# Expert rows by indirect load: empty slots get an index beyond the table instead of row 0

## What is computed

```
g_sel = argmax(g_logits)                 # 1 of 4 groups
top_p, top_i = top_k(softmax(e_logits in that group), 2)
expert = g_sel * 8 + top_i               # 2 experts for each token
gate = t @ w_exp_gate[e]; up = t @ w_exp_up[e]
act = silu(gate) * up * w_tok
out = sum over e of act @ w_exp_down[e]
x = x + gt2 * out
```

## Time and profile before

| | |
|---|---|
| median of 3 runs | 851.57 us (849.39 to 853.31) |
| the profiled execution | 853.74 us |
| its span, first to last instruction | 852.0 us |
| mean granted TensorE clock | 0.93 |
| busy: PE, PEld, DVE, ACT, POOL | 736.1, 534.8, 264.0, 223.6, 97.4 us |
| moved by DMA | 195.88 MB |

### The profile page before, as it was taken

How to read it: one execution, slowest core, us unless ns; L and a number is a source line. 1 busy time by engine, 2 the same in 40 slices (tenths; PEclk the granted TensorE clock), 3 DMA queues, 4 the chain that set the end, 5 groups by cost and what they waited for, 6 DMA issues and landing times.

```text
span 852.0 us, 19975 instructions
## 1 busy us (share of the span) xinstructions
PE 736.1 (86%) x8393; PEld 534.8 (63%) x8394; DVE 264.0 (31%) x737; ACT 223.6 (26%) x523; POOL 97.4 (11%) x229
## 2 busy tenths in 40 slices
PE   2779999999985679999899899983898989989985
PEld 2567777776764457677676677732565656655543
DVE  0035413430135445555561112135111111111132
ACT  1331113123722431252254100151112122121125
POOL 7000000010101330000000000001222222222200
PEclk9769999999996888999999999976899999999996
DMA  7825679998443656315201706874899999999801
GB/s 259 229 96 198 230 261 330 325 327 303 101 115 91 157 150 183 114 51 173 51 26 39 295 0 259 334 295 180 309 411 411 414 413 413 414 412 414 346 14 55
DMA packets 108728, 195.88 MB, mean 230 GB/s; under 512 B 9964, under 2 KB 71097, under 8 KB 100488
## 3 DMA queue, kind: packets, MB, share of 16 engines
q1 hardware_dynamic: 106760, 189.94, 62.2%
q0 software_dynamic: 1920, 5.25, 1.7%
HBM read 185.40 MB, written 9.77 MB: 229 GB/s over the span
## 4 chain that ended last, share of the span: by engine, by line
PE 79%; DVE 7%; ACT 5%; issue 4%; DMA 4%; SPq 1%; DVEq 0%; ACTq 0%; POOLq 0%
PE ps L1110 17%; PE ps L520 10%; PE ps L1268 7%; PE ps L493 5%; PE ps L533 5%; PE ps L438 4%; PE ps L1052 4%; PE ps L417 3%; PE ps L496 3%; PE ps L421 2%; PE ps L483 2%; ACT arena L1496 1%; DMA arena<-in_w_ada 1%; PE ps L527 1%; PE ps L429 1%
## 5 line engine op out<-in xcount | busy, mean ns | idle before, releaser
L1110 PE MATMUL ps<-arena 128*128 128x288 f32 x576 | 144.0, 410 | 0.0
L1110 PEld LDWEIGHTS ps<-arena 128*128 128x128 f32 x576 | 108.9, 191 | 31.1 <-DMA arena<-in_w_in 0.9
L520 PE MATMUL ps<-arena 128*32 128x128 f32 x2432 | 86.5, 278 | 16.0 <-issue 14.0
L520 PEld LDWEIGHTS ps<-arena 128*32 128x32 f32 x2432 | 68.8, 111 | 40.5 <-issue 39.2
L1268 PE MATMUL ps<-arena 128*128 128x288 f32 x256 | 71.8, 425 | 4.1 <-ACT arena L1619 4.1
L1268 PEld LDWEIGHTS ps<-arena 128*128 128x128 f32 x256 | 47.5, 195 | 20.8 <-issue 8.8
L493 PE MATMUL ps<-level,arena 32*128 32x256 f32 x624 | 45.4, 406 | 0.5 <-DVE arena L760 0.5
L533 PE MATMUL ps<-arena,hact 128*32 128x256 f32 x608 | 40.7, 385 | 0.0
L391 POOL DMA_INDIRECT arena<-h_rows,idx_now x38 | 37.5, 987 | 9.5 <-issue 9.5
L755 DVE TENSOR_TENSOR h_row<-h_row,ps 128x64 f32<-128x64 f32 x38 | 8.4, 221 | 97.3 <-ACT h_row L614 97.3
L614 ACT ACTIVATE h_row<-ps 128x64 f32<-128x64 f32 x38 | 8.5, 223 | 111.2 <-PE ps L520 111.2
(11 more groups left out here) (433 smaller groups left out, 1030.7 us busy)
## 6 DMA issues: line engine op xcount, KB each, us to landing
arena<-in_w_exp_gate SPq DMA_DIRECT2D x32, 1024.0 KB
arena<-in_w_exp_up SPq DMA_DIRECT2D x32, 1024.0 KB
arena<-in_w_exp_down SPq DMA_DIRECT2D x32, 1024.0 KB
arena<-in_w_ada SPq DMA_DIRECT2D x12, 2048.0 KB, 10.3
arena<-in_w_in SPq DMA_DIRECT2D x18, 1024.0 KB, 5.7
arena<-in_w_ada_final SPq DMA_DIRECT2D x4, 2048.0 KB, 15.0
arena<-in_w_in SPq DMA_DIRECT2D x16, 512.0 KB
arena<-in_state_ssm_rec SPq DMA_DIRECT2D x8, 512.0 KB, 6.3
```

The source lines that it names most:

```text
L520: l = mm(ps[CW * q:CW * (q + 1), 5, 0:P].rearrange("p (g f) -> p g f", g=2), xwin[:, at:at + CW], gate_up[:, :, k, f:f + HF], start=(k == ...
L1110: l = mm(ps[:, 2 + 2 * sl + m, 0:TOK], w_ring[sl][:, k, m * P:(m + 1) * P], HN[:, k, :], start=(k == 0), stop=(k == KT - 1))
```

## The change

1. tid holds 288 - token, so that the sum of a slot with a token is 288 - token, and of an empty one still 0.
2. DVE computes slot_tab = 288 - sum first: token for a filled slot, 288 for an empty one. It waits for that (link), and computes idx = 4 * slot_tab + quarter from it. An empty slot's index is 1152 to 1155, beyond the last row, 1151.
3. The gather has a bounds_check of 1151 and doesn't take an index beyond it for an error.
4. POOL clears the two buffers once, ahead of y_row, since an empty slot's partition is now not written by a gather. In the first two gathers it holds zeros, and later what an earlier window left there; its weight is 0, and PT has no column 288.

```
-            link(g.iota(tid, pattern=[[0, 2], [P, 3]], base=0, channel_multiplier=1, allow_small_or_imprecise_dtypes=True))
+            link(g.iota(tid, pattern=[[0, 2], [-P, 3]], base=TOK, channel_multiplier=-1, allow_small_or_imprecise_dtypes=True))
...
             e.wait_ge(S("stored"), 16 * rec_stores[0])
+            for xg_ in xgs:
+                link(g.memset(xg_, 0.0))
             g.memset(y_row, 0.0).then_inc(S("y_row"), 1)
             g.memset(PT, 0.0).then_inc(S("pt"), 1)
...
-                g.indirect_dma_start(xgs[u], None, h2_rows, bass.IndirectOffsetOnAxis(rows, 0)).then_inc(S(f"xg_ld{u}"), 16)
+                g.indirect_dma_start(xgs[u], None, h2_rows, bass.IndirectOffsetOnAxis(rows, 0),
+                                     bounds_check=4 * TOK - 1, oob_is_err=False).then_inc(S(f"xg_ld{u}"), 16)
...
             e.wait_ge(S("count_mm"), 2)
-            ts(idx[:], ps[:, 6, 0:NWIN], 4.0, quarter, ALU.mult, ALU.add).then_inc(S("idx"), 1)
-            v.tensor_copy(slot_tab[:, 0, :], ps[:, 6, 0:NWIN])
+            link(ts(slot_tab[:, 0, :], ps[:, 6, 0:NWIN], -1.0, float(TOK), ALU.mult, ALU.add))
+            ts(idx[:], slot_tab[:, 0, :], 4.0, quarter, ALU.mult, ALU.add).then_inc(S("idx"), 1)
```

## The result

The changed kernel takes 855.88 us (median of 6 runs, 854.12 to 856.97) beside 851.05 us for the kernel before: ratio 1.0054, interval 1.0032 to 1.0075. By the ratio it is slower by 4.6 us (the two medians differ by 4.8). The profiled execution has a span of 855.2 us, against 852.0.

The account below looks back on a forecast made before the run. PE's own chain was taken to bound the loop, with the DMA running ahead. The terms 0.2 + 0.1 - 0.17 + 0.3 gave +0.4 us, put on the median as 852.0 us, range 848.5 to 855.8.

Parts of the forecast that it names:

- The loop is not held by the DMA: Loop over windows: the DMA is busy because it runs ahead; 2.9 MB less gather traffic gains nothing there.
- the first rival: Loop: the gathers' traffic held it back through the weights; 7.0 us less, 844.6 us, chance 0.06.
- The loop is PE's own chain: Loop: PE's own work sets the pace, 38 windows of 6.0 us each with the slow first one.
- whatever the check costs in the loop is hidden in POOL's idle time: Loop: extra gather cost from the check is hidden up to about 4.2 us in each window.
- Item 1: Index to first window: idx takes two DVE instructions instead of one, +0.2 us (+0.15 to +0.24).
- Item 2: Index to first window: the bounds check on the first gather, +0.1 us (0 to 0.99).
- Item 3: Index to first window: fewer bytes in the first gather, -0.17 us (0 to -1.0).
- The upper bound of the sum: All terms at their upper bounds: 0.24 + 0.99 + 0 + 0.85 = +2.1 us.
- the slack in the loop: Loop: a gather has 10.3 us to land and the second took 4.4 us, so some 6 us are spare.
- The zeroing: Ahead of the router: two memsets before y_row's delay L449 by 0.8 us, costing +0.3 us (0 to +0.85).
- The clock: Rival: a shifted clock rise or fall makes one window slow or fast, 849.8 or 854.2 us, chance 0.12.
- The other rivals: Gathers: the check makes a slow POOL routine, 887 us at 5 us more, chance 0.08; rows not skipped, 852.2 us, chance 0.08.

Follow-up runs that it names:

- after_idx_direct: The changed kernel with idx made in one instruction and the two buffers cleared behind y_row and PT; ratio 1.0016 to the kernel before.
- before_two_step_idx: The kernel before with DVE's two steps alone (slot_tab first, idx from it), no check, every row loaded; ratio 1.0045 to the kernel before.
- before_gather_late: The kernel before with four small POOL instructions between the wait for idx and the first gather, every row loaded; ratio 1.0036 to the kernel before.
- after: The changed kernel as first measured against the kernel before; 855.88 us, ratio 1.0054.
- after_again: The changed kernel measured once more, beside the follow-up kernels on the same chip; ratio 1.0047 to the kernel before.

## Why the prediction was right or wrong

The forecast was +0.4 us, the sign not clear of nothing; measured is +4.6 us, 0.54%, just outside "within 0.5%", which had the chance 0.83. The median of 855.88 lies at the upper end of the range, 0.1 above 855.8. That end was also added up wrongly: 851.57 + 1.7 + 2.1 is 855.4. That the time came so near the range is luck and no merit of the mechanism: the terms allowed +2.1 us at most, and the rest of the range is the scatter of the runs.

- **The loop is not held by the DMA: right.** The traffic fell as said, and the weights end earlier. With no row at all the loop stays the same, and with 13 us less of PE's time the weights are still not waited for. The 7 us of the first rival are not there.
- **The loop is PE's own chain: wrong in part.** I took the 2.38 us of gate and up for PE's own work, because they are the same under full load and late. Without the gathers they are 1.9: POOL's gathers cost PE 13 us over the loop, and most of it stands in the profile as busy time, while the 14.0 us of "issue" of the earlier trace rows hardly change (13.4). The pauses are in both kernels, so they are no term of the difference, but they are why it failed that whatever the check costs in the loop is hidden in POOL's idle time: the check moves the end of the instruction by some 0.3 us, and the pause with it. In 6 windows gate and up then take 1.86 us instead of 2.4, and the pause falls in the steps behind (from L493 to the down projection: 87.7 us in 37 windows instead of 85.1). These 6 windows get 0.8 us shorter in all; in the 31 others gate and up take 1.9 us more. Why these are longer with the check stays open.
- **Item 1, idx in two steps: right**, 0.23 us for 0.2.
- **Item 2, the check ahead of the first window: right** in size, 0.14 us for 0.1; the 1.2 us in the loop were not in it.
- **Item 3, the first landing: the step that failed.** By itself it is shorter, by 0.37 us (1.97 to 1.60), more than my 0.17. I had taken the mean window for the first one, which moves 0.01 MB and not half of 0.13; by the prediction's own rate, 0.12 MB less are an estimated 0.3 us. But I worked out the terms as if the transfer stood alone. In the changed kernel the delays of items 1 and 2 put the gather behind the load of 1 MB, and the term is +2.17 instead of -0.17: the gather's packets move only behind the load's. The upper bound of the sum, +2.1 us, did not hold for that reason. The load was in the trace, 0.13 us behind the end of the instruction, and I did not ask what stands next in SP's queue; the 4.4 us of the second gather, which I quoted only for the slack in the loop, had the price of it.
- **The zeroing: mechanism right as far as it went, size short.** L449's counterpart ended late, and the router followed it without a gap. The index came 0.69 us later instead of 0.3, inside the bound of 0.85. In this pair of traces the router gives 0.2 us of it (0.4 to 0.5 beside the other traces with ten stretches at half clock). The rest comes from the second fall of the clock, ahead of PE's next step, which I had not looked at. Without the clears ahead of y_row (after_idx_direct) it is back at 36.99 us.
- **The clock:** the pieces ahead of the residual and behind the loop differ by +0.55 and -1.21 us between the two traces; that is scatter of the size that this rival has. The longer and the shorter stretch at half clock around the router, 0.7 us, belong to it too. It explains no difference here that holds over the runs.
- **The other rivals.** The rows are skipped, and the check is no slow routine (0.05 us in the instruction and 0.26 ahead of it).

From the traces, with the check's cost in the loop as the mean over all of them, what stays is 0.69 + 0.23 + 0.14 + 2.17 - 0.14 + 1.2 = 4.3 us, for 4.6 measured.

The Trainium skill ("DMA: Bandwidth & Descriptors", queues, rings and completion order) has each DMA engine take turns between its queues at the grain of a packet. A gather behind the load would then share, and not wait. The runs show otherwise for the landing: in the changed kernel no packet of the gathers moves from 594.0 to 598.2 us, though the first instruction has ended at 595.03. And in the four kernels with the first gather behind the load (before_two_step_idx, before_gather_late, after, after_again) and for the second gather of the kernel before, ACT copies 5.2 to 5.7 us after the load's issue; 1 MB at 413 GB/s is 2.5 us of that. Why the DMA engines do not take turns here stays open.

## What to carry to other kernels

Where a small transfer is on the path, look for the large one that is issued next to it, on any queue, and at how much time decides which comes first: here 0.24 us more on DVE cost over 2 us. A chain of costs that each lie beside nothing is not additive if it moves past such a neighbour. And busy time can hold a pause that another engine causes: gate and up took 2.2 to 2.5 us beside a gather and 1.9 without one, both times as busy time of PE. Where the same instructions take longer in some windows than in others, lay them beside what the other engines do at that moment, before the time is counted as the engine's own.

## What the hardware showed that was not expected

- An indirect gather on POOL holds up PE for some 0.45 us, close behind the end of its instruction (1.0 us), with 128 rows, about 60 on average or none. Without the gathers the loop is 13.1 us shorter (38 gathers, 0.34 us each on average).
- Something of this kind also holds the end of L505 in the kernel before: its modelled end is 592.70, but DVE and SP, which wait for it, go on only at 593.56 and 593.55, just behind the gather's instruction (593.42). In five traces the gather starts 0.34 us or more ahead of that modelled end and SP has no wait of its own; there the load is issued 0.04 to 0.14 us behind the instruction's end; in after, after_again and before_gather_late, where it starts at most 0.15 us ahead, the load is issued 0.05 to 0.06 us behind the modelled end. before_two_step_idx (0.23 us ahead) lies between: the load comes 0.32 us behind the modelled end. So the load comes earlier when the gather comes later. What blocks whom was not tried.
- The landing of a gather alone, from the end of its instruction to ACT's copy: 1.2 us with no row, 1.6 to 1.7 us with 0.01 MB, 1.9 to 2.1 us with all 128 rows of 1 KB (0.13 MB). Behind a load of 1 MB it is 4.1 to 5.0 us, and the gather's packets move only when most of the load's are through.
